# Products of zeros before the waits of a chunkwise matrix inversion, and a convolution rewritten and moved on GpSimd

## The reference: what is computed

```
for l in range(DEPTH):                                   # DEPTH = 2
    z = _rms(h, norm1_g[l]) @ w_in[l]
    ya = _attention_group(za, ...)                       # 8 heads, sinks, windowed over chunks of 64
    yr = _rwkv_group(zr, ...)                            # S = S*w - (S kk)(kk a) + v k, read by r
    yc = _conv_group(zc, ...)                            # causal depthwise convolution of 31 taps, layer norm, silu
    h = h + jnp.concatenate([ya, yr, yc], axis=-1) @ w_out[l]
    h = h + _peer(_rms(h, norm2_g[l]), ...)              # 128 x 128 experts, top 16 of 8 heads
```

## Time and profile before

| | |
|---|---|
| median of 3 runs | 2104.95 us |
| lowest and highest | 2094.97 and 2105.49 us |
| the profiled execution, its own time | 2105.58 us |
| its span, first to last instruction | 2103.4 us |
| mean granted TensorE clock | 0.959 of full speed |
| PE, DVE, POOL, ACT busy share | 94%, 69%, 61%, 46% |

### The profile page before, as it was taken

The page is one execution under the profiler, slowest core; times in us unless marked ns, Lnnn a source line. Parts: engine busy times, 40 slices in busy tenths (PEclk is TensorE's granted clock), DMA queues, the critical chain, the costliest instruction groups (busy, mean ns, idle before and its releaser), DMA issues.

```text
span 2103.4 us, 43605 instructions
## 1 busy us (share of the span) xinstructions
PE 1977.3 (94%) x16516; PEld 1889.8 (90%) x16516; DVE 1459.2 (69%) x2757; ACT 962.2 (46%) x1646; POOL 1279.7 (61%) x667
## 2 busy tenths in 40 slices
PE   9957999999999999999999577999999999999999
PEld 8845899999999999999988467999999999999998
DVE  3864419994777788788748535199627777887886
ACT  5422545554333455545554124455543333555553
POOL 5896469998666633233058964799976666332430
PEclk9966899999999999999999678999999999999999
DMA  5300356665444599899743002566555446998995
GB/s 188 102 1 1 92 170 189 181 180 170 151 143 147 180 339 313 288 313 315 249 135 106 1 1 82 179 192 186 183 169 151 145 146 202 349 322 303 323 328 158
DMA packets 106380, 387.80 MB, mean 184 GB/s; under 512 B 11808, under 2 KB 12064, under 8 KB 106016
## 3 DMA queue, kind: packets, MB, share of 16 engines
q1 hardware_dynamic: 87840, 319.25, 47.3%
q0 software_dynamic: 18432, 67.12, 9.2%
HBM read 385.27 MB, written 1.05 MB: 184 GB/s over the span
## 4 chain that ended last, share of the span: by engine, by line
PE 60%; POOL 24%; issue 13%; DVE 2%; ACT 1%; POOLq 0%; ACTq 0%
PE ps L895 60%; POOL w_lo L552 14%; POOL arena L568 6%; POOL arena L577 4%; DVE x L1386 0%; DVE x_lo L1379 0%; POOL arena L564 0%; ACT w_hi L635 0%; DVE onehots_j L1374 0%; DVE h L1816 0%; DVE sel L1702 0%; ACT L759 0%; ACT L610 0%; DVE h L1815 0%; DVE sel L1705 0%
## 5 line engine op out<-in xcount | busy, mean ns | idle before, releaser
L895 PE MATMUL ps<-x_hi,w_hi 128*128 128x240 f32 (+5 forms) x4768 | 1429.3, 324 | 20.4 <-POOL w_lo L552 10.7
L895 PE MATMUL ps<-x_hi,w_lo 128*128 128x240 f32 (+3 forms) x4768 | 1307.3, 274 | 0.0
L552 POOL TENSOR_TENSOR w_lo<-w,w_hi 128x1024 fp32r<-128x1024 f32 x346 | 871.3, 2536 | 390.6 <-ACT w_hi L635 390.0
L895 PEld LDWEIGHTS ps<-x_hi,w_hi 128*128 128x128 f32 x4768 | 904.2, 190 | 73.5 <-POOL w_lo L552 12.6
L895 PEld LDWEIGHTS ps<-x_hi,w_lo 128*128 128x128 f32 x4768 | 909.3, 191 | 0.0
L635 ACT CAST w_hi<-w 128x1024 fp32r<-128x1024 f32 x596 | 623.5, 1046 | 344.3 <-DMA w<-v_c 204.6
L895 PE MATMUL ps<-x_lo,w_hi 128*128 128x240 f32 (+3 forms) x2720 | 757.1, 278 | 0.0
L895 PEld LDWEIGHTS ps<-x_lo,w_hi 128*128 128x128 f32 x2720 | 519.0, 191 | 0.2
L1773 DVE TENSOR_TENSOR w_lo<-w,w_hi 128x1024 fp32r<-128x1024 f32 x250 | 305.6, 1222 | 114.5 <-ACT w_hi L635 113.7
L895 PE MATMUL ps<-arena 64*64 64x64 f32 (+9 forms) x2496 | 176.7, 277 | 60.9 <-ACT arena L783 19.7
L895 PEld LDWEIGHTS ps<-arena 64*64 64x64 f32 (+6 forms) x2496 | 152.0, 172 | 83.7 <-ACT arena L783 20.4
(11 more groups left out here) (187 smaller groups left out, 1691.7 us busy)
## 6 DMA issues: line engine op xcount, KB each, us to landing
w<-u_c SPq DMA_DIRECT2D x256, 512.0 KB, 3.6
w<-v_c SPq DMA_DIRECT2D x256, 512.0 KB, 5.5
w<-w_c SPq DMA_DIRECT2D x84, 512.0 KB, 3.6
arena<-keys_c SPq DMA_DIRECT2D x2, 1024.0 KB, 5.6
arena<-mix_c SPq DMA_DIRECT2D x2, 792.0 KB, 8.2
h<-h SPq DMA_DIRECT2D x2, 544.0 KB, 4.4
out<-x SPq DMA_DIRECT2D x4, 256.0 KB, 2.1
arena<-lora_c SPq DMA_DIRECT2D x2, 256.0 KB, 9.1
```

What stands on the lines that cost most here:

```text
L552: g.tensor_tensor(low_of(l, n, wlo_t), low_of(l, n, wraw_t), high_of(l, n).bitcast(F32), ALU.subtract).then_inc(s_lo, 1)
L895: return nc.tensor.matmul(out_, lhsT, rhs, start=start, stop=stop, skip_group_check=True)
```

## The change

There are three parts, and a change of PSUM banks that the first of them needs.

First, PE gets a function `fill(n)` that issues n matmuls of 128x128 zeros, added into an otherwise unused part of bank 6. It stands ahead of each wait of the inversion: 2 matmuls before each product x, 4 before each group of updates, so 2 x 2 + 2 x 4 = 12 in a level, 60 in a layer, 120 in all. The second half's update moves from bank 6 to bank 4, from which ACT has by then copied its x.

Second, the convolution's `tensor_scalar` always has two operations, multiply and add; the added number is 0.0 except in the first tap, where it was and is the bias.

Third, POOL starts the convolution after the low half of tile 17 instead of tile 20. The three low halves 18, 19, 20 follow the convolution.

```diff
+IDLE = 2
+UP_BANKS, FILL_BANK = (5, 4), 6
...
-                lows(l, 0 if l == 0 else AHEAD, NZ + AHEAD)
+                lows(l, 0 if l == 0 else AHEAD, NZ)
...
-                                              vcol(l, "conv_b", j) if k == 0 else None, ALU.mult,
-                                              *((ALU.add,) if k == 0 else ()))
+                                              vcol(l, "conv_b", j) if k == 0 else 0.0, ALU.mult, ALU.add)
...
-                lows(l, NZ + AHEAD, NP)
+                lows(l, NZ, NP)
...
+            def fill(n):
+                for _ in range(n):
+                    mm(ps[:, FILL_BANK, NCH * CHUNK:NCH * CHUNK + P], zero_t[:, 0:P], zero_t[:, 0:P], False, True)
...
                 for b in range(nlev):
                     for j in range(2):
+                        fill(IDLE)
                         pe.wait_ge(s_ti, 2 * nlev * l + 2 * b + j + 1)
                         product(3 + j, cm, ti, j).then_inc(s_x, 1)
                     after(steps)
                     for j in range(2):
+                        fill(2 * IDLE)
                         pe.wait_ge(s_xc, 2 * nlev * l + 2 * b + j + 1)
                         pe.wait_ge(s_tt, 2 * (nlev + 1) * l + 2 * b + j + 1)
                         if b < nlev - 1:
-                            product(5 + j, tt_, xm, j).then_inc(s_up, 1)
+                            product(UP_BANKS[j], tt_, xm, j).then_inc(s_up, 1)
...
-                            v.tensor_tensor(ti[:, j], ti[:, j], update(5 + j), ALU.subtract).then_inc(s_ti, 1)
+                            v.tensor_tensor(ti[:, j], ti[:, j], update(UP_BANKS[j]), ALU.subtract).then_inc(s_ti, 1)
```

## The result

The changed kernel took 2117.12 us (median of 8 runs, 2114.82 to 2123.12) against 2103.99 us before (8 runs, 2094.97 to 2106.01). The ratio is 1.0075, 95% interval 1.006 to 1.0091: 13 us slower by the medians and 16 us by the ratio, where 2102 us and no measurable change had been forecast, and outside the range of 2086 to 2112 us. The profiled execution took 2118.78 us, its span 2116.6 us.

The account below looks back on a forecast made before the run. Bound: in the two mixers, 282 us, a cross-engine chain, much PE work at half clock. Zeros +1.4, wait -0.5, contention -2.1 and -1.4 gave -2.6 us: 2103.0 from 2105.6, 2102.4 at the median, said 2102; range 2086 to 2112.

Parts of the forecast that it names:

- Where the time could move: Only the two mixers, 282 us or 13% of the time, can win or lose; PE outside them stays at full clock.
- Which zeros are exposed: Inversion, each layer: 32 of 60 zero products hidden in waits or idle time, 28 exposed on the path.
- Price of an exposed zero and the return of the clock ("net +1.4"): Both layers' inversions: exposed zeros cost 18.7 us, higher clock gives back 17.3 us, net +1.4 us.
- D1: Level 1 of the inversion, the place before the second update: 4 zero products, exposed, priced at half clock, 0.445 us each.
- A2, B2 and C2: Level 2 of the inversion, places before the two x and the first update: 2, 2 and 4 zero products, called hidden.
- The group of 140: 140 PE records at 161.67 in layer 0, 12.54 us: clock up earlier, 5.7 us given back, group at 7 to 8 us.
- Two operations cost nothing but give 0.5 us: POOL's convolution taps: 23.7 us less a layer, of which 0.5 of PE's 2.0 us wait in layer 0 gained.
- would hold DVE up more often while it lasts: Shared SBUF port: the convolution, denser in two-input additions, would block DVE more often; no size given.
- The moved low halves hide behind the rest of the mixer, contention -2.1 us: Low halves after the convolution hide behind the mixer's rest; DVE operations after its earlier end gain 0.8, 1.1 and 0.2 us.
- Start of the mixer, -1.4 us: PE's 0.71 us wait for DVE, slowed by POOL's low halves at the start, goes in both layers: 1.4 us.
- in the way: Rival: in levels 1 to 4 zeros delay released work and the clock does not answer; +21, 2126 us, chance 0.1.

Follow-up runs that it names:

- hidden_zeros: Kernel before plus only the 32 zero products a layer that the forecast called hidden, convolution and low halves as before: 2097.34 us, ratio 0.9994.
- exposed_zeros: Kernel before plus only the 28 zero products a layer that the forecast called exposed, convolution and low halves as before: 2111.47 us, ratio 1.0054.
- zeros_only: Changed kernel with the old multiplications and the old place of the low halves, so all 120 zero products and the bank change: 2109.82 us, ratio 1.0036.
- early_only: Kernel before with the three low halves moved and the bank change, one-operation multiplications, no zeros: 2101.55 us, ratio 1.0001.

## Why the prediction was wrong, point by point

- **Where the time could move**: right. The last stretch has its clock of 0.99 as before, and the two mixers hold the whole loss.
- **Which zeros are exposed**: right, by hidden_zeros and exposed_zeros.
- **Price of an exposed zero and the return of the clock ("net +1.4")**: failed, with a miss of 6.1 us: zeros_only measured +7.5 us. The price was low: 0.46 to 0.50 and 0.27 us, not 0.445 and 0.25, and 21.3 us for the exposed ones, not 18.7. The return was high: by these 21.3 us, an estimate from after's trace, the whole of the zeros gave back 13.8 us, not 17.3. The rate of 0.57 us for each us taken from half clock was itself too high, since of two levels of clock, 1.2 and 2.4 GHz, the higher can save no more than 0.5; at the 0.40 that the text set in brackets the return would have been 12.1 us. In levels 2 and 3 of layer 0 the clock was nearly full (0.94), as forecast, but the stretch from D1's result to the last of level 3 took 20.3 us (131.53 to 151.79) instead of 17.0 (128.30 to 145.33), for in it stood 24 products of zeros, 7.5 us from each fill's start to what follows; the eight of A2, B2 and C2, 2.9 us of it, stood ahead of a wait of 1.89 us, which shrank to 0.55. The group of 140 gave 4.2 us, not 5.7, and the fill ahead of it (172.13 to 173.97) with a 12-record group that now ran at half clock (5.25 us, where 3.46 us at 187.40 before) took most of that back.
- **Two operations cost nothing but give 0.5 us**: failed, and of the same size: the pairs are faster than thought, the wait at the end is gone, and the kernel is 5.2 us slower, where the sum had -0.5 and, with the move, -2.1 us. The text had the mechanism ("would hold DVE up more often while it lasts") and gave it no term. What the runs showed in its place is DVE's time beside the convolution, 46.4 us against 41.1. The profile of before held a hint of its price: DVE's L1418 took 735 ns with all inputs in SBUF, and the same operation and shape with an input from PSUM (L1597) 442 ns.
- **The moved low halves hide behind the rest of the mixer, contention -2.1 us**: half right. L1599's counterpart fell to 0.73 us. But the text did not ask what DVE does from 158 to 165 us, the very time computed for their place.
- **Start of the mixer, -1.4 us**: about right in layer 0 (79.74 against 80.84), small either way; early_only, which has this start, measured 1.0001 in all.
- **Rivals**: the true outcome was nearest to "in the way", 2126 us, though its condition, a clock that does not answer, did not hold. The zeros were in the way with the clock answering. None of the cases had the convolution itself as a loss.

Open: the split of 0.11% between the low halves and scatter, whether the additions alone hold DVE up, and why the clock gave back less than forecast behind the exposed zeros.

## What to carry to other kernels

Filler work on TensorE costs its time wherever the wait behind it has no room for it: put evenly ahead of all waits it lost 0.36%, ahead of the waits with room alone it cost nothing, and sized to long waits it gained 0.25 to 0.4%. A higher mean clock is no gain by itself: it rose from 0.959 to 0.969 in the slower kernel. A faster helper engine is not free: count how often its long instructions meet the chain's operations, not only when it ends. When work is moved in a queue, list what the neighbour engine does at its new time.

## What the runs showed of the hardware that was not expected

- A POOL multiplication 128x272 with one operation took 0.96 us, with two (by a column, plus an immediate 0.0) 0.49 us: the pairs 1.92 and 0.97 us.
- DVE operations on 128x8 took 2.25 to 2.27 us beside POOL's 128x1024 subtractions of 2.32 us, twelve to thirteen times their 0.17 to 0.19 us.
- A POOL memset of 128x544 took 0.55 us. With one in each tap DVE's L1428 took 734 ns, without them 883.
- Four zeros took 1.16 us at full and 1.92 to 2.07 us at half clock, a ratio of about 0.6 and not 0.5. At full clock two took 0.71 us, four 1.16 and 40 in one fill 9.09 us: some 0.22 us for each more, and some 0.27 us that every fill carries once.
